# A backbone layer on one core: x and ctx loaded after the third weight piece, transposes interleaved after the sixth, unit 0 loaded last

## The reference

```python
silu_c, silu_cc = silu(c), silu(c_ctx)
sh1, sc1, g1, sh2, sc2, g2 = split(silu_c @ w_mod + b_mod, 6)      # w_mod is 1024 x 6144
modc = split(silu_cc @ w_mod[:, :2048] + b_mod[:2048], 2)
hc = rmsnorm(ctx, norm1_g) * (1 + modc[1]) + modc[0]
u_ctx = hc @ w_in[:, U_LO:U_HI] + b_in[U_LO:U_HI]                  # only u for the context
ctx_states = ssm_states(u_ctx, lam, log_dt, b, h0=None)            # two scan directions
h = rmsnorm(x, norm1_g) * (1 + sc1) + sh1
z = h @ w_in + b_in                                                # g_b, g_c, x_in, u, gate_a, gate_b
y_a = (g_b * conv3(g_c * x_in)) @ w_out_a
y_b = glu(gelu(ssm(u, h0=final(ctx_states)) + D * u) @ w_glu + b_glu)
x = x + g1 * ((sigmoid(gate_a) * y_a + sigmoid(gate_b) * y_b) @ w_o)
x = x + g2 * swiglu(rmsnorm(x, norm2_g) * (1 + sc2) + sh2)
out = rmsnorm(x, final_g)
```

## Time and profile before

| | |
|---|---|
| median of 3 runs | 582.85 us (582.31 to 584.95) |
| the profiled execution | 582.31 us |
| its span | 580.5 us |
| PE busy | 551.5 us (95%) |
| VectorE busy | 359.4 us (62%) |
| ScalarE busy | 209.6 us (36%) |
| mean DMA rate | 166 GB/s |

### The profile page before, as it was taken

The page is one execution under the profiler, slowest core; times in us unless marked ns, Lnnn a source line. Parts: engine busy times, 40 slices in busy tenths (PEclk is TensorE's granted clock), DMA queues, the critical chain, the costliest instruction groups (busy, mean ns, idle before and its releaser), DMA issues.

```text
span 580.5 us, 8825 instructions
## 1 busy us (share of the span) xinstructions
PE 551.5 (95%) x3502; PEld 447.7 (77%) x3502; DVE 359.4 (62%) x555; ACT 209.6 (36%) x328; POOL 51.1 (9%) x68
## 2 busy tenths in 40 slices
PE   6798999999999999998999969899999999999996
PEld 1127875566666595448999969799999999999995
DVE  5698896373734599992044987568454655554534
ACT  5627241221221011311176545355443344343323
POOL 0011112000000000130001771000000000000000
PEclk9999999999999999999999979989999999999998
DMA  7997977520279242226057964517556464546201
GB/s 280 379 354 241 314 227 242 183 73 1 72 125 101 82 129 72 73 72 218 1 172 263 327 220 154 172 32 260 181 180 207 155 215 150 192 164 217 72 0 72
DMA packets 65578, 96.46 MB, mean 166 GB/s; under 512 B 2304, under 2 KB 54288, under 8 KB 65296
## 3 DMA queue, kind: packets, MB, share of 16 engines
q1 hardware_dynamic: 60368, 78.84, 44.1%
q0 software_dynamic: 4608, 16.78, 8.4%
q10 hardware_dynamic: 576, 0.49, 0.5%
HBM read 94.56 MB, written 1.54 MB: 166 GB/s over the span
## 4 chain that ended last, share of the span: by engine, by line
PE 88%; DMA 4%; DVE 3%; ACT 2%; issue 1%; POOL 1%; SPq 0%; DVEq 0%; ACTq 0%; POOLq 0%
PE bank L1154 24%; PE bank L1232 14%; PE bank L1234 14%; PE bank L1233 14%; PE bank L1132 5%; DMA piece<-in_w_mod 4%; PE bank L1083 3%; PE bank L1177 2%; PE bank L1096 2%; PE bank L1164 1%; PE bank L1221 1%; PE bank L1219 1%; PE bank L1220 1%; PE bank L1208 1%; DVE w_lo L634 1%
## 5 line engine op out<-in xcount | busy, mean ns | idle before, releaser
L634 DVE TENSOR_TENSOR w_lo<-raw,w_hi 128x1024 fp32r<-128x1024 f32 x92 | 112.2, 1255 | 84.6 <-ACT w_hi L516 84.5
L1154 PE MATMUL bank<-hT,raw 128*128 128x256 f32 x288 | 127.5, 611 | 0.0
L1232 PE MATMUL bank<-h_hi,w_hi 128*128 128x256 f32 x432 | 123.2, 285 | 2.8 <-DVE h_lo L637 2.8
L1234 PE MATMUL bank<-h_hi,w_lo 128*128 128x256 f32 x432 | 123.0, 285 | 0.0
L1233 PE MATMUL bank<-h_lo,w_hi 128*128 128x256 f32 x432 | 122.9, 285 | 0.0
L516 ACT CAST w_hi<-raw 128x1024 fp32r<-128x1024 f32 x92 | 94.5, 1047 | 58.1 <-PE bank L1234 58.1
L1154 PEld LDWEIGHTS bank<-hT,raw 128*128 128x128 f32 x288 | 58.4, 206 | 59.6 <-issue 59.3
L1232 PEld LDWEIGHTS bank<-h_hi,w_hi 128*128 128x128 f32 x432 | 83.7, 194 | 3.4 <-DVE h_lo L637 3.2
L1234 PEld LDWEIGHTS bank<-h_hi,w_lo 128*128 128x128 f32 x432 | 83.6, 194 | 0.0
L1233 PEld LDWEIGHTS bank<-h_lo,w_hi 128*128 128x128 f32 x432 | 83.6, 194 | 0.0
L1232 PE MATMUL bank<-a_hi,w_hi 128*128 128x256 f32 x176 | 50.1, 285 | 0.0
(11 more groups left out here) (186 smaller groups left out, 796.3 us busy)
## 6 DMA issues: line engine op xcount, KB each, us to landing
raw<-in_w_ff_in SPq DMA_DIRECT2D x22, 1024.0 KB, 5.0
raw<-in_w_in SPq DMA_DIRECT2D x16, 1024.0 KB, 6.0
piece<-in_w_mod POOLq DMA_DIRECT2D x32, 512.0 KB, 5.6
raw<-in_w_ff_out SPq DMA_DIRECT2D x11, 1024.0 KB, 4.8
piece<-in_w_mod SPq DMA_DIRECT2D x16, 512.0 KB, 6.0
raw<-in_w_glu SPq DMA_DIRECT2D x8, 512.0 KB, 4.1
raw<-in_w_o SPq DMA_DIRECT2D x4, 1024.0 KB, 8.1
xtok<-in_x SPq DMA_DIRECT2D x2, 1024.0 KB, 8.4
```

The source lines that it names most:

```text
L634: return v.tensor_tensor(o, a, b, op)
L1154: last = mm(o, wv[:, k, f * P:(f + 1) * P], rhs[:, k], start=k == 0, stop=k == k_n - 1)
L1232: mm(o, wh, xh, start=first, stop=False, skip_group_check=True)
L1234: return mm(o, wl, xh, start=False, stop=final, skip_group_check=True)
```

## The change

Four edits of the order of work; no operation is added or taken away.

```diff
@@ sync, the loop over the 16 pieces
-            if n == 3:
+            if n == 2:
                 sp.dma_start(xtok[:, 0:2, :], t["x"].rearrange("(a p) d -> p a d", p=P)).then_inc(x_s, 16)
-            if n == 5:
                 sp.dma_start(xtok[:, 2:4, :], t["ctx"].rearrange("(a p) d -> p a d", p=P)).then_inc(ctx_s, 16)
-            if n == 7:
+            if n == 6:
                 sp.dma_start(par_c[:, :, :, :], t["c_pack"]).then_inc(par_c_s, 16)
-            if n == 12:
-                load_unit(0)
-
         sp.dma_start(par_b[:, :, :, :], t["b_pack"]).then_inc(par_b_s, 16)
-        load_unit(1)
+        load_unit(0)
         sp.dma_start(bu[:, :], t["bu_pack"]).then_inc(pack_s, 16)
         sp.dma_start(d_skip[:, :], t["d_pack"]).then_inc(pack_s, 16)
-        for q in range(2, n_pre):
+        for q in range(1, n_pre):
             load_unit(q)
@@ vector
         power(5, 4, 4, 1)
+        dve.wait_ge(S["sqrt_done"], 1)
+        v.reciprocal(rstd[:, :], srow[:, :]).then_inc(S["rstd_ready"], 1)
 
         for d in range(2):
-            if d == 1:
-                dve.wait_ge(S["sqrt_done"], 1)
-                v.reciprocal(rstd[:, :], srow[:, :]).then_inc(S["rstd_ready"], 1)
@@ tensor
-        def xn_cols(k):
-            if k == 0:
-                pe.wait_ge(S["x_scaled"], 4)
+        for n in range(6):
+            mod_part(n)
+        pe.wait_ge(S["x_scaled"], 4)
+        for k in range(KD):
             if k >= 4:
                 pe.wait_ge(S["xn_evac"], k - 3)
             for tt in range(4):
                 last = nc.tensor.transpose(bank[k % 4][:, tt * P:(tt + 1) * P], xtok[:, tt, k * P:(k + 1) * P], ident[:, :])
             last.then_inc(S["xn_mm"], 1)
-
-        for n in range(16):
+            if k % 2:
+                mod_part(6 + k // 2)
+        for n in range(10, 16):
             mod_part(n)
-            if n >= 10:
-                xn_cols(n - 10)
-        xn_cols(6)
-        xn_cols(7)
```

## The result

The changed kernel is slower: 590.35 us (589.0 to 592.72) against 583.9 us for the kernel before, ratio 1.0119 (95% interval 1.0091 to 1.0149). These are medians of four executions each, and they give a ratio of 1.0110; the record lists sixteen executions of the changed kernel, with a median of 591.1 us, and the ratio above lies nearer to that. The direction, the place and the mechanism were as forecast; the size was not. The sum said +4.2 us; +6.45 us were measured by the two medians, +6.9 us by the ratio (0.0119 of 583.9). The 590.35 us lie just inside the range (up to 590.4), the 591.1 us outside it.

The account below looks back on a forecast made before the run. PE's matmul chain was taken as the bound, with the change moving the u projection's start at 50.58 us. +2.6 and +1.6 us gave +4.2 on the median of 582.85, so 587.0 us; range 582.0 to 590.4.

Parts of the forecast that it names:

- The sum: Whole kernel: late unit 0, +2.6 us, plus the clock's fall, +1.6 us, make +4.2 us.
- The shorter tail: End of the mod_parts: three trailing transpose groups gone, mod_rows ready at 46.45 instead of 47.35, hT 0.9 us earlier.
- The first term: Start of the u projection: unit 0 lands late, so it starts at 53.2 instead of 50.58, +2.6 us.
- Three or four POOL pieces: Transfers ahead of unit 0: three POOL pieces land it at 52.55, four at 53.85; 53.2 was taken.
- The price of a piece: Load queue in the head: a piece issued onto a dry queue takes 4.5 us, so piece 15 lands at 42.65.
- The clock in the head: PE before the u projection: mod_parts reckoned at 1.75 us each, piece 15's needed part ending at 38.15.
- The second term: First u projection matmuls: clock falls after 3.7 us of PE idling, +1.6 us, bounds 0 and 2.2.
- The base: Time of the kernel before: median of three executions, 582.85 us, to which +4.2 us was added, giving 587.0.
- A: Head and u projection: unit 0 late and the clock falls, the forecast itself, 585.5 to 588.5 us; chance 0.50.
- B: U projection: unit 0 late but the clock stays up, +2.6 us, 585.5 us; chance 0.15.
- C: U projection: unit 0 there by 49.7, hT decides, -0.9 us, 582.0 us; chance 0.18 with its middle ground.
- D: Head: ctx lands later than 14.1, shifting everything from x_scaled on; 589.0 us if 2 us late; chance 0.17.

Follow-up runs that it names:

- e1: Changed kernel with unit 0 loaded after piece 12 again and unit 1 right behind par_b: 584.5 us, ratio 0.9994.
- e2: Kernel before with only unit 0 moved behind par_b and unit 1 behind d_skip: 586.86 us, ratio 1.0046.
- e7: Changed kernel with PE's loop over mod_part and xn_cols as in the kernel before, SP's and VectorE's edits kept: 584.75 us, ratio 0.9997.
- e4: Changed kernel with POOL's first piece issued only when unit 0 has landed, the other three following: 582.76 us, ratio 0.9961.
- e3: Changed kernel plus five unused 128 x 512 matmuls on PE ahead of the u projection: 588.28 us, ratio 1.0056.
- e14: Kernel before plus sixteen unused small matmuls ahead of the wait for merged rows and ten ahead of h2: 582.85 us, ratio 0.9955.
- e12: Kernel before plus sixteen unused small matmuls behind the wait for merged rows and ten ahead of the first feed-forward product: 587.25 us, ratio 1.0039.
- e15: Changed kernel plus unused matmuls: seven small after mod_part(2), six after mod_part(5), five 128 x 512 ahead of the u projection: 587.88 us, ratio 1.0052.
- e9: Changed kernel plus unused small matmuls: eight after mod_part(2), eight after mod_part(5), six ahead of the mod_rows transposes: 591.57 us, ratio 1.0099.
- e5: Changed kernel plus the small fillers of e9 and the five 128 x 512 matmuls of e3: 587.86 us, ratio 1.0055.
- e13: Changed kernel, eight mod_parts before first transposes, POOL's pieces behind unit 0, fillers ahead of mod_rows transposes, merged-rows wait and h2: 578.83 us, ratio 0.9892.

## Why the prediction was right in kind and too small

**Right.** The loss is unit 0 (e1: put back, 0.9994), by its late place and the new order on PE together: with the old order the late place costs 0.0046 (e2) or nothing that can be measured (e7). It is late because it stands behind piece 15 and par_b, because the 3 us from piece to piece leave the queue dry (159 GB/s against 353), and because POOL's pieces travel at its side (e4). The shorter tail was there too (mod_rows 1.5 us after the last mod_part instead of 3.2), but hT, at 49.8, was later than the 49.0 of before, since the head had lost more ahead of it, and it decided nothing. VectorE was no bound, ctx came at 14.2, and the shift at the end of the head was carried to the end: the first half of the u projection ended 8.1 us later (72.7 against 64.6), the span is 7.7 us longer.

**The first term, +2.6 us.** The changed kernel's profile shows 5.3 us. Three steps of it were off.

*Three or four POOL pieces.* "I take 53.2" lay between the two; four give 53.85. Every profile with unit 0 last and POOL's pieces free shows four ahead of it. The rule cited there from the Trainium skill ("DMA: Bandwidth & Descriptors", "Queues, rings and completion order"), that each engine goes round between the queues that have work, had given +3.3 us. The trace agrees with it: POOL's fourth piece was issued 6.9 us after unit 0 and landed 1.6 us before it.

*The price of a piece.* "A piece issued onto a queue that has run dry takes 4.5 us" misreads the row: when that piece was issued, at 28.12, the queue was full. The pieces of the changed kernel that were issued onto a dry queue, at 27.21 and 30.22 (0 GB/s in 27 to 28 us, 16 in 30 to 31), took 3.4 us.

```profile
24.00:28.00 4.00, 2.50 (x7) 0.42 (x6) 3.83 (x11) 3.94 (x4) 0.00 (x0) 1.00 1.02 412
```

```profile
piece<-in_w_mod SPq DMA_DIRECT2D x1, 512.0 KB, 3.4
```

Piece 15 was not one of these. With piece 14 just ahead of it and par_b and unit 0 right behind, it took 5.5 us, and 4.7 to 6.5 in the other profiles with unit 0 last and POOL's pieces free.

*The clock in the head.* It was taken to be 1.0 throughout, at no cost. In the changed kernel's profile a mod_part at half clock (1.5 us) helped to put the issue of piece 15 at 39.3 instead of 38.15. e3's profile has no such fall.

With the clock held up, e3's ratio of 1.0056 is 3.3 us of 585, and e3's profile has the u projection 53.83 - 50.58 = 3.25 us later. By these the term was 0.6 us small. But 50.58 is an early start of the kernel before (52.07 and 52.22 in e14 and e12), and e3's filler may itself run over in some executions, as e15's did. So the lateness of unit 0 by itself is known to about 1.5 us only, and so is the second term, which is the rest.

**The second term, +1.6 us.** By the medians this is the step that failed most: the price of the clock's fall. It cost 2.9 us in the profile, and 1.0119 - 1.0056 = 0.0063, 3.7 us, by the ratios of the changed kernel and e3 (with both intervals, 1 to 6 us; e9 and e5 give 2.6). I took it "near the row" after 2.81 us of idle time. The idle time that I had just forecast, 3.7 us, and all the more the 4.66 us that came, was nearer to another wait of PE in the kernel before, of which the prediction shows no row:

```profile
342.96 0.55 PE L1232 MATMUL bank<-m_hi,w_hi 128*128 128x256 f32 x1 [4.50 <-DVE yb L637]
```

```profile
340.00:342.00 2.00, 0.00 (x0) 0.00 (x0) 0.95 (x3) 1.09 (x2) 0.80 (x2) 0.63 1.06 369
342.00:344.00 2.00, 1.04 (x5) 1.07 (x6) 1.97 (x4) 1.69 (x3) 1.51 (x2) 0.50 0.32 71
344.00:346.00 2.00, 2.00 (x11) 2.00 (x11) 2.00 (x2) 0.01 (x1) 1.92 (x3) 0.50 0.68 238
346.00:348.00 2.00, 2.00 (x14) 2.00 (x13) 1.91 (x2) 0.40 (x1) 1.92 (x2) 0.67 0.65 215
```

The clock was low there for 6.8 us, 2.4 of them inside the wait and 4.4 in work, which costs 2.2 us: my upper bound. After the wait for unit 0 it was low in work for about 5.7 us. So that stretch would have brought the term nearer, but not to 2.9; why the low clock lasted longer here stays open.

**A slip without effect.** mod_part(0) to (2) end at 9.74 + 2 x 1.75 = 13.24 by the prediction's own numbers, not at 13.1 (13.7 came); piece 3, at 15.4, decided.

**The base.** The prediction of 587.0 us started from a median of three executions, 582.85. The kernel before has a median of 585.1 in the 35 and 33 executions of the first two jobs, and 583.9 with the changed kernel. Part of its spread goes with the clock: of the 35 executions (582 to 590 us), the twelve with a mean granted clock of 0.984 or more have a median of 583.6 us, the five with 0.973 or less 588.6. The distance of forecast and measured time, 3.35 us, is thus 1.05 us of base and 2.3 us of the two terms; by the ratio the terms missed 2.7 us.

**The rivals.** A came true beyond its upper end of 588.5. B did not: the clock fell, and the 3 us that it names are no bound, since rows 10 and 11 show a fall after 2.81 us. C needed unit 0 by 49.7, and with unit 0 last that came only where POOL's pieces were held back (48.95 in e4); there h_cols(0) at half clock kept the start at 50.58. D, a late ctx, did not happen.

## What to carry to other kernels

A load that nobody waits for can still be filling a gap; before it is moved back, look at what the queue carries in the stretch it leaves, and at every other queue that will be busy where it arrives. The waits of PE of 2.8, 4.5 and 4.7 us were paid twice here, once as a wait and once in the matmuls after it, and matmuls whose results nobody reads, put inside the wait (never behind it), gave the second part back. When a forecast of a few microseconds rests on three executions, their median is one of its errors.

## What the runs showed that I had not expected

How much of the time goes with the clock. The mean granted clock was 0.984 in the profiled execution before (median 0.981 in 35 others), and 0.97 to 0.976 in all but one of sixteen executions of the changed kernel (0.965). e13, with fillers in three waits, has the highest (median 0.992 over its six executions) and the lowest time. A small filler of 128 x 128 matmuls was enough to hold the clock at 1.0 through a stretch of 4.7 us in which PE had nothing else to do (339.52 to 344.20 in e13, 3.74 us of it filler). Short waits of 1.4 to 2 us in the head were followed by a fall in some profiles (the changed kernel's, at 24 us) and not in others (e3's), with the same code there; ahead of the mod_rows transposes, 1.70 us were followed by h_cols(0) at half clock in e7 and at full clock in the kernel before.
